# The last four units of an output projection in Strassen's form

## What is computed

```
def layer(x, ...):
    h = rms(x, norm_mix)
    proj = h @ w_in                       # split among 4 head groups of 256 channels
    y_a ... y_d                           # recurrence, attention, retention, mLSTM
    x = x + concat([y_a, y_b, y_c, y_d]) @ w_out      # 1024 x 1024: the output projection
    gu = rms(x, norm_ffn) @ w_gu          # 1024 x 5632
    x = x + (silu(gu[:, :2816]) * gu[:, 2816:]) @ w_down
    return x, (h_new, conv_new, S_new, C_new, n_new, m_new, ...)   # the new states are outputs too
```

## Time and profile before

| | |
|---|---|
| median of 3 runs | 907.32 us (907.29 to 907.59) |
| the profiled execution | 907.33 us |
| its span | 905.5 us, so 1.8 us lie around it |
| TensorE busy | 894.2 us, 99% of the span |
| VectorE, GpSimd, ScalarE busy | 522.5, 512.6, 220.3 us |
| DMA | mean 125 GB/s |
| granted TensorE clock | 1.0 in every slice |

### The profile page before, as it was taken

How to read it: one execution, slowest core, us unless ns; L and a number is a source line. 1 busy time by engine, 2 the same in 40 slices (tenths; PEclk the granted TensorE clock), 3 DMA queues, 4 the chain that set the end, 5 groups by cost and what they waited for, 6 DMA issues and landing times.

```text
span 905.5 us, 15566 instructions
## 1 busy us (share of the span) xinstructions
PE 894.2 (99%) x5980; PEld 815.2 (90%) x5980; DVE 522.5 (58%) x1032; ACT 220.3 (24%) x485; POOL 512.6 (57%) x514
## 2 busy tenths in 40 slices
PE   8999999999999999999999999999999999999998
PEld 6997878668999999999979878876799999999998
DVE  6677858835656565522366776685465656563221
ACT  3334355532000000100133433464300000000001
POOL 6851573226866666666457244912287666666770
PEclk9999999999999999999999999999999999999999
DMA  9979322248445454344444873121855555443421
GB/s 272 259 128 113 100 65 77 53 90 230 140 140 141 140 139 130 128 128 129 129 134 141 31 152 95 48 87 17 183 140 140 140 140 140 140 129 128 147 87 35
DMA packets 159091, 112.92 MB, mean 125 GB/s; under 512 B 9829, under 2 KB 156682, under 8 KB 158890
## 3 DMA queue, kind: packets, MB, share of 16 engines
q1 hardware_dynamic: 154402, 104.44, 40.2%
q0 software_dynamic: 3984, 6.74, 7.3%
q10 hardware_dynamic: 632, 0.75, 0.3%
HBM read 108.33 MB, written 2.27 MB: 122 GB/s over the span
## 4 chain that ended last, share of the span: by engine, by line
PE 94%; DVE 3%; ACT 1%; issue 1%; DMA 1%; SPq 0%; DVEq 0%; ACTq 0%
PE ps L1315 53%; PE ps L865 8%; PE ps L1272 7%; PE ps L899 7%; PE ps L885 3%; PE ps L1333 2%; PE ps L1085 2%; PE ps L1054 1%; PE ps L1117 1%; PE ps L1218 1%; PE ps L1210 1%; DMA arena<-in_x_sample 1%; PE ps L973 1%; DVE work L2081 1%; PE ps L1011 1%
## 5 line engine op out<-in xcount | busy, mean ns | idle before, releaser
L674 POOL TENSOR_TENSOR work<-ring 128x512 f32<-128x512 f32 (+1 forms) x66 | 81.8, 1240 | 154.6 <-issue 113.3
L1315 PE MATMUL ps<-mixT,ring 128*128 128x160 f32 x672 | 105.0, 299 | 0.0
L1315 PE MATMUL ps<-hT,work 128*128 128x160 f32 x672 | 98.5, 299 | 0.0
L1315 PE MATMUL ps<-hT,ring 128*128 128x160 f32 x672 | 98.1, 299 | 0.0
L1315 PEld LDWEIGHTS ps<-mixT,ring 128*128 128x128 f32 x672 | 95.8, 190 | 0.0
L1315 PEld LDWEIGHTS ps<-hT,ring 128*128 128x128 f32 x672 | 93.7, 190 | 0.3
L1315 PEld LDWEIGHTS ps<-hT,work 128*128 128x128 f32 x672 | 93.7, 190 | 0.0
L675 POOL TENSOR_TENSOR ring<-ring 128x512 f32<-128x512 f32 (+1 forms) x66 | 82.4, 1249 | 5.2
L676 POOL TENSOR_TENSOR work<-ring 128x512 f32<-128x512 f32 (+1 forms) x66 | 82.2, 1246 | 5.2
L677 POOL TENSOR_TENSOR work<-ring,work 128x512 f32<-128x512 f32 (+1 forms) x66 | 81.9, 1241 | 5.2
L1766 ACT ACTIVATE arena<-ps 128x160 f32<-128x160 f32 x42 | 12.8, 304 | 286.8 <-PE ps L1315 286.8
(11 more groups left out here) (447 smaller groups left out, 1630.6 us busy)
## 6 DMA issues: line engine op xcount, KB each, us to landing
ring<-in_w_gu SPq DMA_DIRECT2D x88, 512.0 KB, 5.2
ring<-in_w_in SPq DMA_DIRECT2D x44, 512.0 KB, 7.2
ring<-in_w_down SPq DMA_DIRECT2D x32, 512.0 KB, 4.5
ring<-in_w_out SPq DMA_DIRECT2D x16, 512.0 KB, 4.7
ring<-in_w_down SPq DMA_DIRECT2D x16, 384.0 KB, 3.7
cst<-in_consts POOLq DMA_DIRECT2D x1, 1664.0 KB, 11.4
ring<-in_w_in SPq DMA_DIRECT2D x2, 640.0 KB, 5.8
arena<-r POOLq DMA_DIRECT2D x8, 160.0 KB, 18.0
```

The source lines that it names most:

```text
L674: step(tt(s3, a11, a21, ALU.subtract))
L1315: ins = mm(bank(use, at * HT, HT), left, right(k), start=(opens and k == 0 and at == 0), stop=(closes and k == n - 1), skip_group_check=True)
```

## The change

Units 4 to 7 of the output projection are no longer plain. Chunks o2 and o3 (`OUTS`) each become one Strassen pair of 7 products over 4 pairs of `mixT` tiles. Their weight sums stand at the head of GpSimd's list of chunks, ahead of f1. VectorE makes four sums of `mixT` tiles (`msum`, semaphore `mix_sums`) right behind the last tile of `mixT`, and adds the pairs to `xT` in `out_pair`, eight operations a pair. ScalarE copies one product of each pair out of PSUM (`p1_copied`). Products 1, 2 and 3 of pair 2 and products 1 and 2 of pair 3 are begun early on tiles 6, 7, 2 and 3, where `project(4, ...)` and `project(5, ...)` stood.

```
-MIXES = FT - 1 + 3 * NQ
+OUTS = (2, 3)
+MIXES = len(OUTS) + FT - 1 + 3 * NQ
...
-    u += [(f"o{n}", (n,)) for n in range(KT)]
+    u += [(f"o{n}", (n,)) for n in range(4)]
+    u += [("p2a", (4,)), ("p2c", (5,)), ("p3a", (6,)), ("p2b", (0,)), ("p3b", (1,)), ("p3c", (7,))]
...
-        MIX_CHUNKS = [f"f{j}" for j in range(1, FT)] + [f"y{q}_{r}" for q in range(NQ) for r in range(3)]
+        MIX_CHUNKS = [f"o{i}" for i in OUTS] + [f"f{j}" for j in range(1, FT)] + [f"y{q}_{r}" for q in range(NQ) for r in range(3)]
...
                 if i == 1:
+                    need(pool, "mix_sums", l, 4)
+                elif i == len(OUTS) + 1:
                     need(pool, "h_sums", l, 4)
...
-                project(4, (6, 7, 2, 3))
+                def out_product(p, which, ks, opens=False, closes=False):
+                    i = OUTS.index(p)
+                    use = f"p{p}" + {1: "a", 2: "a", 6: "a", 5: "b", 7: "b", 3: "c", 4: "c"}[which]
+                    if opens:
+                        claim(pe, use, l)
+                    wait_chunk(pe, f"o{p}", l)
+                    if which in (3, 5, 6, 7):
+                        need(pe, "mixed", l, MADE, NPAIR + i + 1)
+                    if which in (4, 5, 6, 7):
+                        need(pe, "mix_sums", l, 4)
...
+                early, late, every = (3, 1), (2, 0), (3, 1, 2, 0)
+                out_product(2, 1, early, opens=True)
+                out_product(2, 2, early)
+                out_product(2, 3, early, opens=True)
                 need(pe, "h_sq", l, 1)
                 for t in range(2):
                     claim(pe, f"am{t}", l)
                     fill(mm(bank(f"am{t}", 0, AW), C("headmean"), an[:, t, :], start=True, stop=True), f"am{t}")
-                project(5, (6, 7, 2, 3))
+                out_product(3, 1, early, opens=True)
+                out_product(3, 2, early)
                 for n in range(2):
                     project(n, (0, 1))
                 for n in range(2):
                     project(n, (4, 5))
-                for n in range(2, 6):
+                for n in range(2, 4):
                     project(n, (0, 1, 4, 5))
-                for n in range(6, KT):
-                    project(n, (6, 7, 2, 3, 0, 1, 4, 5))
+                out_product(2, 1, late)
+                out_product(2, 2, late)
+                out_product(2, 3, late)
+                out_product(2, 6, every, closes=True)
+                out_product(2, 5, every, opens=True)
+                out_product(2, 7, every, closes=True)
+                out_product(2, 4, every, closes=True)
+                out_product(3, 1, late)
+                out_product(3, 2, late)
+                out_product(3, 6, every, closes=True)
+                out_product(3, 5, every, opens=True)
+                out_product(3, 7, every, closes=True)
+                out_product(3, 3, every, opens=True)
+                out_product(3, 4, every, closes=True)
...
-                squares(l, 1)
+                squares(l, 1, range(4))
+                for p in OUTS:
+                    need(act, "x_new", l, 2 * KT, 2 * p)
+                    wait_filled(act, f"p{p}a", l)
+                    step(A(pair_p1, bank(f"p{p}a", 0, HT), ACT.Copy), "p1_copied")
+                    squares(l, 1, range(2 * p, 2 * p + 2))
...
+                m_at = lambda j, t: mixT[:, j::2, t * HT:(t + 1) * HT]
+                step(v.tensor_tensor(msum[0], m_at(0, 1), m_at(0, 0), ALU.subtract), "mix_sums")
+                step(v.tensor_tensor(msum[2], m_at(1, 1), msum[0], ALU.subtract), "mix_sums")
+                step(v.tensor_tensor(msum[1], m_at(1, 1), m_at(0, 1), ALU.subtract), "mix_sums")
+                step(v.tensor_tensor(msum[3], m_at(1, 0), msum[2], ALU.subtract), "mix_sums")
...
+                for p in OUTS:
+                    squares_so_far(2 * p)
+                    out_pair(p)
+                    squares_so_far(2 * p + 1)
```

More of the change, by code:

```diff
@@ L64 @@
 NPAIR = len(PAIRS)
-MIXES = FT - 1 + 3 * NQ
+OUTS = (2, 3)
+MIXES = len(OUTS) + FT - 1 + 3 * NQ
 MADE = NPAIR + MIXES
-P1S = NPAIR + FT - 1 + NQ
+P1S = NPAIR + len(OUTS) + FT - 1 + NQ
 MSLOTS = 3
@@ L198 @@
             "rk": "rk1", "rg": "rgc", "rv": "rvc", "lx": "lx1", "lg": "lg1"}
-LAST_USE.update({f"o{i}": f"o{2 * i + 1}" for i in range(4)})
+LAST_USE.update({f"o{i}": f"p{i}c" if i in OUTS else f"o{2 * i + 1}" for i in range(4)})
 LAST_USE.update({f"f{j}": f"fc{j}" if j else "fb0" for j in range(FT)})
@@ L342, in build @@
         xgm = mixT
+        low = MSLOTS * 3 * 512 + KT * T
+        msum = [x.rearrange("p (k n) -> p k n", n=HT) for x in
+                (work[:, low:low + 4 * HT], work[:, low + 4 * HT:low + 8 * HT], work[:, low + 8 * HT:low + 12 * HT],
+                 pT[:, 0:4 * HT])]
         hp = mixT[:, :, :].rearrange("p k n -> p (k n)").rearrange("p (s k n) -> p s k n", s=4, k=4)
@@ L1289, in _ @@
                 pair_mean(1, l)
-                project(4, (6, 7, 2, 3))
+                def out_product(p, which, ks, opens=False, closes=False):
[8 more added lines that the diff above has]
+                        need(pe, "mix_sums", l, 4)
+                    w, _ = quarters(f"o{p}", l)
+                    at = {1: 0, 2: 2, 6: 1, 5: 0, 7: 1, 3: 0, 4: 1}[which]
+                    for k in ks:
+                        need(pe, f"mix{k}", l, 1)
+                        left = {1: w[:, k, 0, 0, :], 2: w[:, k, 1, 0, :], 3: sums[:, i % MSLOTS, 2, k, :],
+                                4: w[:, k, 1, 1, :], 5: w[:, k, 0, 1, :], 6: sums[:, i % MSLOTS, 0, k, :],
+                                7: sums[:, i % MSLOTS, 1, k, :]}[which]
+                        right = {1: mixT[:, 2 * k, 0:HT], 2: mixT[:, 2 * k + 1, 0:HT], 3: mixT[:, 2 * k + 1, HT:T],
+                                 4: msum[3][:, k, :], 5: msum[0][:, k, :], 6: msum[2][:, k, :], 7: msum[1][:, k, :]}[which]
+                        ins = mm(bank(use, at * HT, HT), left, right, start=(opens and k == ks[0]), stop=(k == 0),
+                                 skip_group_check=True)
+                    if closes:
+                        fill(ins, use)
+                early, late, every = (3, 1), (2, 0), (3, 1, 2, 0)
+                out_product(2, 1, early, opens=True)
+                out_product(2, 2, early)
+                out_product(2, 3, early, opens=True)
                 need(pe, "h_sq", l, 1)
@@ L1404, in _ @@
                     for r in range(3):
-                        i = FT - 1 + 3 * q + r
+                        i = len(OUTS) + FT - 1 + 3 * q + r
                         wait_chunk(pe, f"y{q}_{r}", l)
@@ L2303, in _ @@
                     if n > 1:
-                        need(dve, "squared", l, 2 * KT, KT + n)
-                        step(v.tensor_tensor(hT[:, 0, 0:T], hT[:, 0, 0:T], hT[:, n - 1, 0:T], ALU.add),
-                             "sq_seven" if n == KT - 1 else None)
+                        squares_so_far(n)
+                for p in OUTS:
+                    squares_so_far(2 * p)
+                    out_pair(p)
+                    squares_so_far(2 * p + 1)
                 need(dve, "rstd", l, 2, 2)
@@ L2334, in gate_up @@
                     p1 = p1c[:, j % 2, :]
-                    need(dve, "p1_copied", l, P1S, NPAIR + j)
+                    need(dve, "p1_copied", l, P1S, NPAIR + len(OUTS) + j)
                     step(v.tensor_tensor(u2, p1, bank(fa, HT, HT), ALU.add))
@@ L2372, in _ @@
                     mid = xT[:, 2 * q:2 * q + 2, :].rearrange("p k n -> p (k n)")[:, HT:3 * HT]
-                    need(dve, "p1_copied", l, P1S, NPAIR + FT + q)
+                    need(dve, "p1_copied", l, P1S, NPAIR + len(OUTS) + FT + q)
                     step(v.tensor_tensor(u2, p1, bank(ya, HT, HT), ALU.add))
```

43 lines of the change are left out of this document (33 added, 10 removed).

## The result

The changed kernel takes **964.84 us** (964.18 to 964.90) against 907.46 us (907.29 to 907.76), a ratio of 1.0631 with an interval of 1.0618 to 1.0644. The profiled execution has a span of 961.9 us, 56.4 more than before.

What follows compares the result with a forecast made beforehand. TensorE's program plus its waits was taken to bound the kernel. Terms -4.1 + 51.3 + 2.1 + 3.0 gave +52.3 us on about 907.3, so 959.6, stated as 960 us, range 953 to 967.

Steps and rivals of the forecast that it cites:

- The saving, -4.1 us: Output projection on TensorE: short Strassen matmuls replace plain ones, saving 1.02 us a pair, two pairs in each of two layers.
- The wait, +51.3 us: TensorE at product 3 of pair 2 waits for GpSimd's o2 sums behind the state writes: 26.7 and 24.6 us.
- the landing of the writes: GpSimd's state writes, without f1's load beside them, were taken to land 2.0 us earlier, from a range of 0 to 3.8.
- The lost cover, +2.1 us: Between am0 and mix0, short matmuls replace plain ones, leaving TensorE 1.07 us more idle in each layer.
- The clock, +3.0 us: After each layer's long wait TensorE restarts at a slower clock, 1.5 us for each of two restarts.
- VectorE's sums, hidden: VectorE's four mixT sums behind mix0 end before TensorE wants them, hidden by 5.9 us; o3's sums by 9.9.
- The end of the projection: Last square ready 2.5 us after the last product, hidden by 2.7 us of f0 matmuls; could cost 1 us a layer.
- The writes that land soon (935): Rival: state writes land much sooner, waits of only 14.2 and 12.2 us, 935 us; chance 0.09.
- The forecast's far case, 969: No earlier landing, clock slow twice as long, projection's end uncovered: 969 us; chance 0.86 together with forecast and its other ends.
- The other side (905.3, sums ready in time): Rival: o2's sums are ready when product 3 asks, only -2.0 us left, 905.3 us, faster; chance 0.01.

Runs made afterwards that it cites:

- experiment 11: Experiment 9 with GpSimd's sums of f1 waiting until VectorE has added the last pair to xT: 907.79 us, 1.0007 of the kernel before.
- experiment 4: Changed kernel without the four convolution-state writes in each layer, the recurrence-state writes kept: 945.05 us in one execution.
- experiment 12: Experiment 11 with group a's mixT tiles first again and products 1 and 2 of pair 3 late again: 909.54 us, 1.0023 of the kernel before.
- experiment 3: Changed kernel with 46 matmuls of 320 columns, their result overwritten, put into TensorE's wait in each layer: 963.66 us, 1.0622 of the kernel before.
- experiment 8: Experiment 6 with group c first, f0's second bank claimed only where used, late parts of pair 3's products 1 and 2 moved ahead: 917.96 us.
- experiment 2: Changed kernel with GpSimd's o2 sums made after group c's first state and o3's before the wait for the state writes: 924.66 us, 1.0175.
- experiment 6: Changed kernel with o2 and o3 sums after VectorE's four sums, between issuing and awaiting state writes, and pair 2's product 3 late: 916.34 us.
- experiment 9: Experiment 8 with the convolution-state writes moved early, to near 146 us, right behind the rotations: 910.43 us, 1.0032 of the kernel before.
- 5: Experiment 2 without any of the eight convolution and recurrence state writes in each layer: 917.70 us, 1.0114 of the kernel before.
- 1: Changed kernel with product 3 of pair 2 done whole behind the plain units and not early: 943.61 us, 1.0400 of the kernel before.
- 7: Kernel before, plain form, with mixT tiles 4 and 5 (group c) written and multiplied ahead of 0 and 1: 906.28 us, 0.9989.

## Why the prediction was right

Forecast 960 us, measured 964.84, in the range. By its steps:

*The saving, -4.1 us.* Right. In experiment 11, where TensorE waits for nothing between `am0` and f0, 16 plain and 52 short matmuls and `am0` and `am1` take 202.26 - 177.92 = 24.3 us: 16 x 0.540 and 52 x 0.272 make 22.8, and the 1.49 us from `am0` to the first short one nearly all the rest.

*The wait, +51.3 us.* The mechanism was right: the row, the releaser and both places. Measured 28.29 + 26.35 = 54.6 us. The term that was mis-sized is the landing of the writes: I took 2.0 us earlier of a range of 0 to 3.8, and it was 15.52 - 15.29 = 0.23 us in layer 0. In layer 1 the last issue ended at 654.02 and the sums began at 669.45, 15.43 us where I had 13.5. That is 1.8 + 1.9 = 3.7 us. The working that failed is the step that let the writes land earlier by part of the share that the load took: with the load gone they landed as before. What sets their time is open, as experiment 4 says. The Trainium skill (DMA: Bandwidth & Descriptors, Rules for kernel authors) says that a write whose last dimension is strided becomes one descriptor for each element. No trace here shows that: it counts 256 packets for the 2048 elements.

*The lost cover, +2.1 us.* Right. It shows as 1.10 and 0.69 us of idle time in front of the first matmul behind `mix0`. At the full clock it is 1.10 in both layers (experiment 12), whose rows give the 1.07 us a layer.

*The clock, +3.0 us.* Right in kind, mis-sized by a little: from product 3's start to the first matmul behind `mix0` it took 210.60 - 204.98 = 5.62 and 5.63 us, where 5.98 were forecast (0.54 + 3.94 + 1.5). At a granted clock of 1.00 it is 4.46 us, in layer 1 of experiment 3. So the slow clock costs 1.2 us a layer, not 1.5. That the kernel's own start gave a price so near was in part luck: the same 24 records take 5.49 us in the trace after, by which the price would have been 2.7.

*VectorE's sums, hidden.* Right: nothing waits for `mix_sums` or for o3's sums.

*The end of the projection, "hidden, but only just".* The last square was in time, as said. What I had not seen is a claim: f0 opens two banks at its start, and TensorE stands 0.60 and 0.59 us there. Experiment 8, which claims the second bank later, has no wait at this place. From `mix0` on it took 232.55 - 210.60 = 21.95 us, where 21.1 were forecast. That is 0.85 us in each layer, 0.60 of it this claim.

The errors of these terms are 3.7 for the landing and 1.7 for the projection's end, with 0.7 back for the clock: 4.7 us too little. The measured time is 4.8 above the 960, but that the two agree so well is in part chance. The span of the profiled execution grew by 56.4 us where 52.3 were forecast, so 4.1, and the rest of the 4.7 came back between the two layers' projections (from f0 in layer 0 to product 1 in layer 1 it is 647.38 - 232.55 = 414.83 us, 415.35 in the kernel before), for which I have no reason.

*The rivals.* The writes that land soon (935) fell: nothing in the windows moves while they are out, but they are out. Its argument from the DMA share failed, since the packets are counted near their issue and the landings come up to 15 us later. The forecast's far case, 969, lay beyond the stated range of 953 to 967, which the prediction gives no reason for. The other side (905.3, sums ready in time) needed GpSimd's chain turned round; experiments 2, 6, 8, 9 and 11 did that step by step, and none of them is faster. That was wrong in the rival: it left 2.0 us of gain after the lost cover, and the runs found none, for the idle time in front of `am0` and the late, slowed sum of squares at f0 take the rest.

## What to carry to other kernels

Before an early product is given a new operand, look up what the engine that makes the operand is doing at that time: here 1 us of arithmetic saved a pair put TensorE behind a receipt of 2048 single elements. A form with fewer matmuls also gives less cover, so at each place where the long form hid a chain of other engines, subtract what becomes visible, and bank claims too; with 2 us to win a layer, two such places (1.07 us in front of `am0`, 1.40 at f0) were enough. And here the writes of single elements were best issued long before anything on that queue or on other engines was urgent: moving three quarters of them gave 7.5 us (experiment 9).

## What the runs showed of the hardware that was not expected

- Eight writes of single elements, 2048 in all, had landed 20.4 us after their first issue, and four writes with 512 after 9.6 us. The profile counts 256 packets for the 2048, all before 184 us, and a DMA share of 0.00 for the last 12 us.
- While 2048 such elements were out and the core was busy, VectorE or ScalarE stood for 2.8 to 6.9 us with no cause in the records (experiments 2, 6, 8), and in no run with 512 or none beside the projection (5, 9, 11, 12). In the kernel before, and in 1, 3 and 7, nothing of this was seen in spite of 2048 elements. In layer 0 each such stall ended 1.0 to 1.6 us before GpSimd went on behind its wait for the writes (203.69 and 204.69, 199.04 and 200.06, 197.76 and 199.40). Why is open. The Trainium skill (Runtime: NRT & Kernel Launch, Instruction fetch mechanics) has engines load their instructions by DMA in blocks, so a block's load behind the writes was a candidate. The records speak against it: during none of the six stalls do the queues that carry instructions have a packet (in experiment 8, from 190 to 198 us, only the queue of the weights has any).
- VectorE and GpSimd slow each other: 0.83 to 1.65 and 0.50 to 1.45 us on VectorE, 1.27 to 1.83 on GpSimd (experiment 2), 0.49 to 1.31 for a single sum (experiment 11). The Trainium skill (Trainium Architecture — The Big Picture, What this means for kernel authors) calls their common port a lock and not a split. The numbers show that both lose time, and don't tell the one from the other.
- The granted clock fell to 0.50 after short rests of TensorE too: 4.3 us (experiment 3, layer 0, `am0` in 2.36 us), 3.24 us (experiment 6), and 2.34 us behind shorter ones (experiment 2, `am0` in 2.52 us). After 28 us of rest `am0` took 2.14 us. It stayed at 1.00 after 1.25 us (experiment 3, layer 1, `am0` in 1.25 us) and after 2.30 us (experiment 9).
